# RWKV state of two heads as diagonal blocks of one 128x128 square, and no products with the zero state

## The reference

```python
def step(state, inp):
    r_t, w_t, k_t, v_t, kk_t, a_t = inp
    sa = jnp.einsum('bhij,bhj->bhi', state, -kk_t)
    state = (state * w_t[:, :, None, :]
             + sa[..., None] * (kk_t * a_t)[:, :, None, :]
             + v_t[..., None] * k_t[:, :, None, :])
    y_t = jnp.einsum('bhij,bhj->bhi', state, r_t)
    return state, y_t
state0 = jnp.zeros((b, RWKV_HEADS, HEAD_DIM, HEAD_DIM), jnp.float32)
_, y = lax.scan(step, state0, xs)
```

## Time and profile before

| | |
|---|---|
| median of 3 runs | 2015.48 us (2014.5 to 2015.75) |
| the profiled execution | 2015.33 us, span 2013.5 us |
| TensorE busy | 1915.0 us, 95% of the span |
| VectorE, ScalarE, GpSimd busy | 879.9, 760.4, 513.3 us |
| mean granted TensorE clock | 0.968 of full |
| pair steps with a pair in its chunks | about 367 to 869 us of the span |

### The profile page before, as it was taken

One profiled execution on the slowest core, in us unless ns is written; L12 is line 12 of the kernel. 1 busy time (PEld: TensorE's weight loads), 2 busy tenths in 40 slices (PEclk: granted clock), 3 DMA queues, 4 the chain that ended last, 5 costly groups with the idle time before them and its releaser, 6 DMA issues.

```text
span 2013.5 us, 24217 instructions
## 1 busy us (share of the span) xinstructions
PE 1915.0 (95%) x10404; PEld 1568.8 (78%) x10404; DVE 879.9 (44%) x1337; ACT 760.4 (38%) x1099; POOL 513.3 (25%) x115
## 2 busy tenths in 40 slices
PE   7999878999999999989899999989999999999998
PEld 5887656778777877868788888878776788888886
DVE  2015436677768765523511334450784331112344
ACT  4225534345444543423422222342565242222222
POOL 2422200000000000014243443423332524434432
PEclk9999988899999988999899999989999999999999
DMA  4712131000110000144232232322122222232321
GB/s 149 246 64 63 58 91 38 24 25 22 34 33 27 22 22 26 44 162 146 74 105 90 99 105 85 104 88 93 60 84 70 98 94 86 103 104 85 105 93 75
DMA packets 54511, 160.77 MB, mean 80 GB/s; under 512 B 3296, under 2 KB 30304, under 8 KB 39685
## 3 DMA queue, kind: packets, MB, share of 16 engines
q1 hardware_dynamic: 42476, 135.40, 20.1%
q10 hardware_dynamic: 11928, 23.83, 3.5%
HBM read 152.63 MB, written 10.25 MB: 81 GB/s over the span
## 4 chain that ended last, share of the span: by engine, by line
PE 85%; DVE 6%; ACT 6%; issue 2%; DMA 1%; POOL 0%; ACTq 0%; DVEq 0%
PE ps L572 23%; PE ps L573 22%; PE ps L574 21%; PE ps L956 2%; PE ps L966 2%; PE ps L964 2%; PE ps L996 1%; PE ps L993 1%; PE ps L1044 1%; ACT w_hi L1219 1%; PE ps L688 1%; PE ps L973 1%; PE ps L1006 1%; DVE level L1961 1%; DVE x_res L1772 1%
## 5 line engine op out<-in xcount | busy, mean ns | idle before, releaser
L563 POOL TENSOR_TENSOR w_lo<-w_raw,w_hi 128x2048 fp32r<-128x2048 f32 x111 | 513.1, 4623 | 1470.1 <-ACT w_hi L1219 1470.1
L572 PE MATMUL ps<-ht_hi,w_hi 128*128 128x512 f32 (+1 forms) x1304 | 531.6, 408 | 17.1 <-DVE ht_lo L1758 8.7
L573 PE MATMUL ps<-ht_lo,w_hi 128*128 128x512 f32 (+1 forms) x1304 | 503.5, 386 | 0.0
L574 PE MATMUL ps<-ht_hi,w_lo 128*128 128x512 f32 (+1 forms) x1304 | 503.2, 386 | 0.0
L1219 ACT ACTIVATE w_hi<-w_raw 128x2048 fp32r<-128x2048 f32 x126 | 240.9, 1914 | 489.3 <-PE ps L574 437.5
L572 PEld LDWEIGHTS ps<-ht_hi,w_hi 128*128 128x128 f32 x1304 | 251.9, 193 | 83.7 <-issue 34.0
L574 PEld LDWEIGHTS ps<-ht_hi,w_lo 128*128 128x128 f32 x1304 | 251.1, 193 | 49.2
L573 PEld LDWEIGHTS ps<-ht_lo,w_hi 128*128 128x128 f32 x1304 | 252.5, 194 | 39.3 <-issue 2.2
L2167 DVE TENSOR_TENSOR hid_lo<-hidden,hid_hi 128x1024 fp32r<-128x1024 f32 x27 | 129.3, 4788 | 149.1 <-ACT hid_hi L1584 149.1
L572 PE MATMUL ps<-w_hi,hid_hi 128*128 128x512 f32 x432 | 168.4, 390 | 0.0
L573 PE MATMUL ps<-w_lo,hid_hi 128*128 128x512 f32 x432 | 168.3, 390 | 0.0
(11 more groups left out here) (290 smaller groups left out, 2643.4 us busy)
## 6 DMA issues: line engine op xcount, KB each, us to landing
w_raw<-in_wpack SPq DMA_DIRECT2D x114, 1024.0 KB, 4.8
w_raw<-in_wpack SPq DMA_DIRECT2D x24, 512.0 KB, 5.4
bias_skewed_dram<-bias_rows_dram ACTq DMA_DIRECT2D x1, 3840.0 KB, 23.0
toe<-bias_skewed_dram ACTq DMA_DIRECT2D x1, 3072.0 KB, 13.0
x_res<-in_x SPq DMA_DIRECT2D x4, 512.0 KB, 5.8
merged<-gate_dram ACTq DMA_DIRECT2D x1, 2048.0 KB, 10.6
gate<-gate_dram ACTq DMA_DIRECT2D x1, 2048.0 KB, 12.7
x_res<-in_x ACTq DMA_DIRECT2D x1, 2048.0 KB, 9.2
```

What stands on the lines that cost most here:

```text
L563: nc.gpsimd.tensor_tensor(Wl[:, slot, :], raw[:, slot, :], f32(Wh[:, slot, :]), ALU.subtract).then_inc(lo_ready, 1)
L572: mm(dst, wh, ah, start=first, stop=False)
L573: mm(dst, wh, al, start=False, stop=False)
L574: return mm(dst, wl, ah, start=False, stop=last)
```

## The change

`S` becomes a full 128x128 square with the two heads' states as diagonal blocks. `chunk_rhs` multiplies it in one product with all 128 rows, and again in one for the output; `head_done` falls away. `chunk_out` forms the new part of the state as two products of 128x128, which hold the cross terms of the two heads as well, and VectorE's scaling multiplies by `ones_head` (one on the diagonal blocks, zero elsewhere), which puts the cross terms to zero. In chunk 0 the products with the zero state are left out, the gram products begin the sum instead, there is nothing to add to, and `state_zero` goes with its wait. The wider `S` takes the room of the tiles `LM` and `NR`, which move to another region.

```diff
@@ -281,14 +281,14 @@
         RKV = r("rkv", [P, 2, 3, T])
         GT = r("gate1_tile", [P, T])
         identR = r("ident_r", [P, P], F32R)
-        S = r("state", [P, HD])
+        S = r("state", [P, P])
         RH = r("rhs_sb", [P, P])
         SA = r("sa_sb", [P, P])
-        LM = r("mid_decay", [P, 2, 2, NT])
-        NR = [r(f"root{i}", [P, NT, 2]) for i in range(2)]
         assert r.at <= y_at + 4 * NT * D
         r = Region(base)
         LW = [r(f"lora_w{i}", [P, 2, P]) for i in range(2)]
+        LM = r("mid_decay", [P, 2, 2, NT])
+        NR = [r(f"root{i}", [P, NT, 2]) for i in range(2)]
         RA = [r(f"ra{i}", [P, NT, 2, P]) for i in range(2)]
         BON = [r(f"bonus{i}", [P, T]) for i in range(2)]
         Gb = [r(f"rwkv_gate{i}", [P, T]) for i in range(2)]
@@ -390,7 +390,7 @@
             "z_full", "sig_ready", "zg_full", "g_ready", "sq_ready", "ss_full", "nrm_ready", "rn_ready", "rnx_ready", "rb_full",
             "kk_ready", "rk_ready", "bonus_full", "bon_ready", "csm_ready", "exps_ready", "xexp_ready", "ra_ready",
             "kb1_ready", "kb_ready", "tok_full", "tok_ready", "agram_full", "gram_full", "gram_taken", "m_ready",
-            "x_full", "x1_ready", "tt_full", "t_ready", "t2_ready", "s_ready", "head_done", "rhs_full", "rhs_ready", "sa_full",
+            "x_full", "x1_ready", "tt_full", "t_ready", "t2_ready", "s_ready", "rhs_full", "rhs_ready", "sa_full",
             "sa_ready", "s_full", "y_full", "yraw_ready", "mu_full", "ysq_ready", "var_full", "std_ready",
             "rv_ready", "rvx_ready", "rvb_full", "rvm_ready", "u_full", "e_ready", "c_full", "tf_ready")}
 
@@ -981,22 +981,20 @@
                     inc(last, "c_full")
 
 
             def chunk_rhs(a, t):
                 ra = RA[a % 2]
-                w("s_ready", NT, a, t + 1)
                 if t == 0:
                     w("tok_ready", 3, a, 3)
                     w("gram_taken", NT, a, NT)
+                else:
+                    w("s_ready", NT - 1, a, t)
+                    mm(ps[:, 3, 0:P], ra[:, t, 1, :], S[:], start=True, stop=False)
                 for h in range(2):
-                    if h:
-                        w("head_done", NT, a, t + 1)
-                    first = mm(ps[:, 3, heads(h)], ra[heads(h), t, 1, :], S[heads(h), :], start=True, stop=False)
-                    if h == 0:
-                        inc(first, "head_done")
-                    last = mm(ps[:, 3, heads(h)], GM[h][:, t, 1, :], TV[:, t, heads(h)], start=False, stop=True)
+                    last = mm(ps[:, 3, heads(h)], GM[h][:, t, 1, :], TV[:, t, heads(h)], start=t == 0, stop=t == 0 or h == 1)
                 inc(last, "rhs_full")
-                for h in range(2):
-                    mm(ps[heads(h), 2, tok(t)], S[heads(h), :], ra[heads(h), t, 0, :], start=True, stop=False)
+                if t:
+                    mm(ps[:, 2, tok(t)], S[:], ra[:, t, 0, :], start=True, stop=False)
 
             def chunk_solve(a, t):
                 if t == 0:
@@ -1009,13 +1007,11 @@
             def chunk_out(a, t):
                 w("sa_ready", NT, a, t + 1)
                 if t < NT - 1:
-                    for h in range(2):
-                        mm(ps[heads(h), 3, 2 * P:2 * P + HD], TB[:, t, heads(h)], SA[:, heads(h)], start=True, stop=False)
-                        last = mm(ps[heads(h), 3, 2 * P:2 * P + HD], TK[:, t, heads(h)], TV[:, t, heads(h)],
-                                  start=False, stop=True)
+                    mm(ps[:, 3, 2 * P:3 * P], TB[:, t, :], SA[:], start=True, stop=False)
+                    last = mm(ps[:, 3, 2 * P:3 * P], TK[:, t, :], TV[:, t, :], start=False, stop=True)
                     inc(last, "s_full")
                 for h in range(2):
-                    mm(ps[heads(h), 2, tok(t)], TV[:, t, heads(h)], GM[h][:, t, 0, :], start=False, stop=False)
+                    mm(ps[heads(h), 2, tok(t)], TV[:, t, heads(h)], GM[h][:, t, 0, :], start=t == 0, stop=False)
                     last = mm(ps[heads(h), 2, tok(t)], SA[:, heads(h)], GM[h][:, t, 2, :], start=False, stop=True)
                 if t == NT - 1:
                     inc(last, "y_full")
@@ -1997,14 +1993,13 @@
                 inc(v.tensor_copy(SA[:], ps[:, 3, P:2 * P]), "sa_ready")
 
             def state(a, t):
+
                 w("s_full", NT - 1, a, t + 1)
-                order(v.tensor_tensor(S[:], ps[:, 3, 2 * P:2 * P + HD], S[:], ALU.add))
-                inc(v.tensor_scalar(S[:], S[:], LM[:, a % 2, 1, t:t + 1], None, ALU.mult), "s_ready")
-
-            def state_zero(b):
-                if b:
-                    w("y_full", 1, b - 1, 1)
-                inc(v.memset(S[:], 0.0), "s_ready")
+                new = ps[:, 3, 2 * P:3 * P]
+                if t:
+                    order(v.tensor_tensor(S[:], new, S[:], ALU.add))
+                    new = S[:]
+                inc(v.scalar_tensor_tensor(S[:], new, LM[:, a % 2, 1, t:t + 1], ones_head, ALU.mult, ALU.mult), "s_ready")
 
             def grams(b, t):
                 w("gram_full", NT, b, t + 1)
@@ -2118,7 +2113,6 @@
                     bonus(c)
                 if has_b:
                     refine_t(b)
-                    state_zero(b)
                 if has_c:
                     keys(c)
```

## The result

| | |
|---|---|
| changed kernel, median of 4 runs | 1985.79 us (1981.58 to 1989.06) |
| kernel before, 4 runs beside them | 2014.99 us (2011.51 to 2015.75) |
| ratio | 0.9855, 95% interval 0.9842 to 0.9868 |
| profiled execution | 1984.22 us, span 1982.4, mean granted clock 0.970 |

What follows compares the result with a forecast made beforehand. TensorE was taken to bound the pair steps. Five steps at 2.9 us (14.5), the first 3.3, the one at 773 3.9 and the last 2.5 sum to 24.2 us: 1991.3 us, range 1984.5 to 2000.

Steps and rivals of the forecast that it cites:

- the surplus: Right-hand side, chunks 1 to 3: 0.09 to 0.14 us extra where neighbouring products use different array parts; gain 1.0 us each.
- The update, 0.16 dearer: State update, 24 chunks: two full products in place of four 64-column ones cost TensorE 0.16 us more each, 3.8 us.
- VectorE: State add and scaling: chunk 0 0.15 us shorter, other chunks 0.15 us longer, counting only where VectorE leads.
- term (a): Chunk 1 of a pair step: VectorE's start moves less than TensorE's, beyond 0.6 us of slack, so 0.1 us is lost.
- Chunk 0: Zero-state products and memset wait go: L944 1.26 us sooner in five steps, 1.8 in the first, 1.4 in two.
- term (b): Chunk 3: the fill unit waits for the shifted half from ScalarE's copy and VectorE's shift, so 0.8 us is lost.
- the step at 773: Pair step starting at 773 us, without a fill waiting for the shift: chunk 0 gives 1.4 us, the step 3.9.
- Rival 1: Pair steps: all of TensorE's gain gets through, 31 us, giving 1984 us; chance 0.10.
- Rival 2: Pair steps: the VectorE and ScalarE chain takes the lead, gain about 13 us, giving 2002 us; chance 0.15.
- Rival 3: Right-hand sides: the surplus belongs to every change of destination, 8.6 us stays, giving 1999.7 us; chance 0.03.
- Rival 4: Tile rule holds: right-hand sides gain nothing, update loses 3.8 us, dropped zero products give 3.5; 2015.6 us; chance 0.01.
- Rival 5: Pair steps: the granted clock falls in six more steps, costing 30.6 us, giving 2022 us; chance 0.02.

Runs made afterwards that it cites:

- e3: The changed kernel with the output's product with the state again as two 64x64 tiles; 1991.31 us, ratio 0.9885.
- e2: The kernel before (state in two halves, tiled products) with only the products with the zero state left out; 1992.66 us, ratio 0.9896.
- e4: The changed kernel with the state update formed in four tiles as before, VectorE placing each head's block; 1981.07 us, ratio 0.9835.
- e5: The changed kernel with ScalarE's copy of the shifted half ahead of the key roots' table load in the first five pair steps; 1984.46 us, ratio 0.9851.
- e0: The changed kernel run again without any edit; 1985.69 us, ratio 0.9854.
- e9: e8 with ScalarE's weight unit moved behind its right-hand side copy in two pair steps, and six idle products in the sixth; 1976.95 us, ratio 0.9816.
- e8: The changed kernel with the edits of e4 and e5 plus idle TensorE products; 1981.94 us, ratio 0.9846; again 1980.89 us, ratio 0.9833.

## Why the prediction was right, and 5 us short

**TensorE sets the pace and the surplus is the change of form: right.** The right-hand side takes 1.70 in place of 2.75 us, 1.05 for the 1.0 taken. e3 and e2 show the cause by themselves.

**The update, 0.16 dearer: right in size on TensorE** (1.35 against 1.19), in effect 0.03 to 0.13 a chunk (e4).

**VectorE:** the add takes 0.292 and the scaling 0.352 us, where 0.29 and 0.343 were taken. Where it could be felt, in chunk 1 (term (a), 0.1 a step), one of the steps has a wait of L964 for L1979, 0.24 us, and the others none.

**Chunk 0: undersized.** L944 comes 1.43 to 1.46 us sooner behind the step before, where 1.26 was worked out; first 1.73 (1.8), at p6 1.29 (1.4). The working had 0.45 us for the four records and 0.20 behind them for the step to 64 rows. They take 0.48 with that step in it (496.53 to 497.01). The other limit, the end of L1952 at 496.94, lies just ahead of L944 and costs nothing.

**Chunk 3's fill, term (b), 0.8 lost: right where it is.** The wait is there in p0 to p4, 0.47 to 0.57 us, on top of the little that was there before. e5 takes it away. But the step from 704 to 771 was counted with 2.9 like the others, and in it no fill waits for a shift. It gave 67.6 - 63.5 = 4.1 us at the same clock of 0.92. The prediction treated the step at 773 so, and not this one: here its working was wrong, by 1.2 us. (In e0 the same step ran at 0.90 and gave 2.3, so the 1.2 hold for this profile.) Of the others p6 gave 4.3 for 3.9, the first 3.2 for 3.3 (its own terms, 1.8 + 3.0 - 0.48 - 0.1 - 0.8, make 3.4), the last 2.6 for 2.5.

**The clock's level was left out of the sum.** At the full clock a step of the p2 kind went from 66.6 us (p2 before) to 63.5 (p4 after), and p3, at 0.97 in both, from 67.1 to 64.0: 3.1 for 2.9, and the 0.2 is chunk 0's. But p1 and p4 were at 0.97 before and at 1.00 after, p2 the reverse, and the four steps together gave 67.2 + 66.6 + 67.1 + 67.6 - 62.8 - 64.3 - 64.0 - 63.5 = 13.9 us for 11.6. Chunk 0 is 0.8 of these 2.3. The remaining 1.5 are the clock's: 1.3 more in p1, 1.0 more in p4, 0.8 less in p2.

**"Everything behind the pair steps only starts sooner": right for the instructions, wrong for the time of a profile.** The part behind was 2.8 us shorter in this profile, at a granted clock of 0.99 for 0.98, and 0.2 longer in e0's, at 0.98.

Together: 2.3 in p1 to p4, 1.2 in p5, 0.4 in the others make 28.1 out of 24.2 in the chunk part. So the mechanism was right. Of the 3.9 us in the chunk part 2.4 are terms of the sum (p5's fill, chunk 0 and the small ones), 1.5 the clock's level, and what the medians have beyond that lies outside it. Nothing here shows that the change has a hold on the clock's level; the median, 1985.79, lies 1.3 us above the lower end of the range, so that the range held is in part luck. With 2.8 behind and 0.2 ahead of it the two profiled executions stand 31.1 us apart (2015.33 and 1984.22), the medians 29.2.

**The rivals.** Rival 1 (31 us, 1984) came near in the number, but not by its mechanism: (b) is not soft, it waits in p0 to p4; (a) did turn out nearly soft, with one wait in all. Rival 2 took no lead: the wait for the level masks fell from 4.4 to 2.2 us. A milder form of it came true, the wait for ScalarE's copy of the right-hand side, 1.1 to 5.8 us; e9 cut it to 2.5. Rival 3 fell with e3. Rival 4, the tile rule of the Trainium skill (TensorEngine Tiling, Theoretical Speedup), fell by rows and runs: with tiles (e2) the chunk part is 16 us longer. For the update alone, where small products follow one another in one form, tiles are the faster ones (e4). The Trainium skill (TensorEngine Tiling, Key Properties) says that changing the tiling mode drains the array; the 0.09 to 0.14 us of the earlier trace rows at each change of form agree. Rival 5 did not happen: the granted clock rose in p1, p4 and p6 and fell in p2 and, by 0.01, in p0.

## What to carry to other kernels

Read a product's price from start to start, and beside the neighbours it has in the program: small tiles between full-array products lost 0.09 to 0.14 us at each change of form, and multiplying in zeros of a block-diagonal square was cheaper. Then, when the bounding engine has been made shorter, list its waits again: two of those that grew hung in part on the order of ScalarE's work, and changing it gave 0.7 to 0.8 us in the even steps p0, p2 and p4 and 1.2 in the odd ones p1 and p3. And work out the gain of each step from what that step contains: the one without the waiting fill gave a third more than its neighbours.

## What the runs showed of the hardware beyond that

- Halving the moving columns of a full-array fp32 product saved nothing: L994's four records with 64 columns take 0.40 us up to L997, 0.20 for each product, and L997's two with 128 take 0.19.
- Additional TensorE work in front of a wait can make a kernel faster: 22 idle products, 7.6 us busy, gave 4.5 to 5.9 us in the chunk part, because p1 to p4 and p6 held the full granted clock.
- The part behind the chunks, the same instructions in all kernels, took from 1135.4 to 1140.6 us in the thirteen profiles. It goes with the granted clock there: the six profiles with 0.98 took 1138.7 to 1140.6 us, the seven with 0.99 took 1135.4 to 1138.4. What decides it was not found: e8 had 1140.6 twice, while the changed kernel had 1137.5 and 1140.5. A gain below 3 us should be read in its own stretch, and not in the total alone. Equally open is why p2 of e9 fell to 0.95.
